# Attention values made transposed on two column tiles, with GpSimd scaling the probabilities

## The reference, cut to what matters

```python
h = x @ w_in                                   # 256 x 3080
prob = softmax(q @ k.T * hd**-0.5 + bias)      # or + c_t - c_s, causal
o = prob @ v                                   # per head, 256 x 64
return concat(o) @ w_out                       # 1024 x 1024
```

## Time and profile before

| | |
|---|---|
| median of 3 runs | 1023.72 us (1022.42 to 1024.78) |
| profiled execution, own time | 1023.21 us |
| its span | 1021.7 us |
| TensorE busy in the span | 1012.8 us (99%) |
| VectorE, ScalarE, GpSimd busy | 610.1, 448.5, 41.9 us |
| mean granted clock | 0.999 |

### The profile page before, as it was taken

One profiled execution on the slowest core, in us unless ns is written; L12 is line 12 of the kernel. 1 busy time (PEld: TensorE's weight loads), 2 busy tenths in 40 slices (PEclk: granted clock), 3 DMA queues, 4 the chain that ended last, 5 costly groups with the idle time before them and its releaser, 6 DMA issues.

```text
span 1021.7 us, 12789 instructions
## 1 busy us (share of the span) xinstructions
PE 1012.8 (99%) x4816; PEld 836.2 (82%) x4816; DVE 610.1 (60%) x716; ACT 448.5 (44%) x523; POOL 41.9 (4%) x55
## 2 busy tenths in 40 slices
PE   9999999999999999999999999999999999999998
PEld 7888888888888888888888888888887888888887
DVE  5655455776478745454677544545778864545574
ACT  5444344346473643434356343434344553434441
POOL 0400000100000000000010000000210100000010
PEclk9999999999999999999999999999999999999999
DMA  8875656355236766565539656564467676465531
GB/s 289 283 230 177 208 171 210 114 178 172 83 110 220 250 204 205 164 205 164 165 128 321 210 165 206 165 212 156 135 194 238 204 250 206 164 207 171 196 124 42
DMA packets 129683, 191.47 MB, mean 187 GB/s; under 512 B 5448, under 2 KB 95816, under 8 KB 129520
## 3 DMA queue, kind: packets, MB, share of 16 engines
q1 hardware_dynamic: 126432, 180.11, 53.9%
q0 software_dynamic: 2928, 10.61, 3.1%
q10 hardware_dynamic: 288, 0.26, 0.1%
HBM read 189.90 MB, written 1.06 MB: 187 GB/s over the span
## 4 chain that ended last, share of the span: by engine, by line
PE 93%; DVE 4%; DMA 1%; ACT 1%; issue 1%; SPq 0%; DVEq 0%; ACTq 0%
PE gu L388 19%; PE gu L390 19%; PE gu L389 19%; PE acc L388 10%; PE acc L390 10%; PE acc L389 10%; PE tp L466 4%; DVE g_lo L1118 2%; DMA rawB<-in_sgu_w_in 1%; ACT g_hi L830 1%; PE acc L653 1%; DVE t_tok L1514 0%; DVE xT_lo L1118 0%; DMA x_tok<-in_x 0%; DVE stage L1505 0%
## 5 line engine op out<-in xcount | busy, mean ns | idle before, releaser
L388 PE MATMUL gu<-g_hi,xT_hi 128*128 128x512 f32 x928 | 363.5, 392 | 1.2 <-DVE xT_lo L1118 1.1
L390 PE MATMUL gu<-g_hi,xT_lo 128*128 128x512 f32 x928 | 361.0, 389 | 0.0
L389 PE MATMUL gu<-g_lo,xT_hi 128*128 128x512 f32 x928 | 360.4, 388 | 0.0
L388 PEld LDWEIGHTS gu<-g_hi,xT_hi 128*128 128x128 f32 x928 | 174.3, 188 | 37.5 <-issue 2.4
L390 PEld LDWEIGHTS gu<-g_hi,xT_lo 128*128 128x128 f32 x928 | 174.2, 188 | 36.2
L389 PEld LDWEIGHTS gu<-g_lo,xT_hi 128*128 128x128 f32 x928 | 174.3, 188 | 34.8
L896 ACT ACTIVATE stage<-gu 128x256 f32<-128x256 f32 x88 | 33.7, 383 | 361.2 <-PE gu L390 361.1
L1118 DVE TENSOR_TENSOR g_lo<-rawA,g_hi 128x2048 fp32r<-128x2048 f32 (+2 forms) x66 | 141.5, 2145 | 78.4 <-ACT g_hi L830 78.3
L1118 DVE TENSOR_TENSOR g_lo<-rawB,g_hi 128x2048 fp32r<-128x2048 f32 (+1 forms) x64 | 141.0, 2203 | 18.1 <-ACT g_hi L830 18.1
L1244 DVE SCALAR_TENSOR_TENSOR stage<-stage,gu 128x256 f32<-128x256 f32 x88 | 37.0, 420 | 189.6 <-ACT stage L896 189.6
L388 PE MATMUL acc<-d_hi,hT_hi 128*128 128x512 f32 x352 | 144.8, 411 | 0.0
(11 more groups left out here) (181 smaller groups left out, 673.1 us busy)
## 6 DMA issues: line engine op xcount, KB each, us to landing
rawD<-in_ffn_w_down SPq DMA_DIRECT2D x44, 1024.0 KB, 4.9
rawA<-in_ffn_w_gate SPq DMA_DIRECT2D x42, 512.0 KB, 4.0
rawA<-in_ffn_w_up SPq DMA_DIRECT2D x42, 512.0 KB, 4.9
rawB<-in_ffn_w_gate SPq DMA_DIRECT2D x42, 512.0 KB, 4.4
rawB<-in_ffn_w_up SPq DMA_DIRECT2D x42, 512.0 KB, 5.5
rawA<-in_attn_w_in SPq DMA_DIRECT2D x12, 512.0 KB, 4.4
rawB<-in_attn_w_in SPq DMA_DIRECT2D x12, 512.0 KB, 4.9
rawA<-in_ple_w_gate SPq DMA_DIRECT2D x8, 512.0 KB, 4.7
```

The lines of the kernel that those rows point to most:

```text
L388: pe.matmul(dst, hi[b], w_hi[b], start=first and b == 0, stop=False)
L389: pe.matmul(dst, hi[b], w_lo[b], start=False, stop=False)
L390: done = pe.matmul(dst, lo[b], w_hi[b], start=False, stop=last and b == len(hi) - 1)
```

## The change

Four things change.

1. `values` works on a pair of heads at once and swaps the operands: v (64 columns) is stationary and the turned probabilities (128 columns) move, so the result stands transposed, head 2p in rows 0 to 63 and head 2p+1 in rows 64 to 127. It is 6 matmuls of 64x128 a pair, alternating between the two column tiles, where it was 6 of 128x64. The result goes straight into `oT_hi`, `oT_lo` (MoBA) and `xT_hi`, `xT_lo` (FoX) by `outputs`, so `group_out`, `o turn` and `oT` go, and with them 16 transposes on TensorE.
2. The row sums can then no longer be applied to the result. For each pair VectorE makes the reciprocals (`inverse`) and GpSimd multiplies the probabilities in place, two instructions a head, before TensorE turns them. `probs_turn` waits for GpSimd (`scaled`) and not for ScalarE (`p_ready`).
3. Where a product of h = 1 follows a transposition, it starts with 8 of its matmuls that need only `xT_hi` (`g_product_high_first`).
4. In sgu, VectorE's order around `gate_y` changes. `ATTN_ORDER` is rewritten to fit.

```diff
     ("g", 4, 0), ("probs", 2), ("probs", 3), ("scores", 2), ("exps", 2), ("turn", 3, 1), ("values", 1),
+    ("outputs", 0, 0), ("inverse", 2),
...
+        with ExitStack() as region:
+            oT_hi = sb("oT_hi", [P, HEADS, S], F32R, region)
+            oT_lo = sb("oT_lo", [P, HEADS, S], F32R, region)
...
+            def g_product_high_first(slot, dst, high_use, operand_wait):
+
+                tok = slice(P, 2 * P)
+                pe.wait_ge(tp_hi[0], high_use)
+                for b in range(4):
+                    pe.matmul(dst, xT_hi[:, b, tok], g_hi[:, slot, b, :], start=b == 0, stop=False)
+                    pe.matmul(dst, xT_hi[:, b, tok], g_lo[:, slot, b, :], start=False, stop=False)
+                operand_wait(0, 1)
+                for b in range(4):
+                    pe.matmul(dst, xT_lo[:, b, tok], g_hi[:, slot, b, :], start=False, stop=False)
+                operand_wait(1, 1)
+                g_piece(slot, 1, dst, 4, KB).then_inc(g_done, 1)
...
                     def probs_turn(n):
-                        pe.wait_ge(p_ready, n + 1)
+                        pe.wait_ge(scaled, n + 1)
...
-                        pe.matmul(o[0][:, oc], probsT[:, sl, 2 * P:3 * P], v_att[:, 0, vc],
-                                  start=True, stop=True)
-                        pe.matmul(o[1][:, oc], probsT[:, sl, 0:P], v_att[:, 0, vc], start=True, stop=False)
-                        pe.matmul(o[1][:, oc], probsT[:, sl, P:2 * P], v_att[:, 1, vc],
-                                  start=False, stop=True).then_inc(pv_done, 1)
+                        o = heads_out[g][p % 4 // 2]
+                        for q, keys, part in ((0, 0, 2), (1, 0, 0), (1, 1, 1)):
+                            for r in range(2):
+                                vc = slice(P * p + HD * r, P * p + HD * r + HD)
+                                done = pe.matmul(o[HD * r:HD * r + HD, at + P * q:at + P * q + P],
+                                                 v_att[:, keys, vc], probsT[:, r, P * part:P * part + P],
+                                                 start=keys == 0, stop=keys == q)
+                        done.then_inc(pv_done, 1)
...
+                        elif e[0] == "outputs":
+                            g, b = e[1:]
+                            src, hi, _ = outputs_of(g, b)
+                            act.wait_ge(pv_done, 4 * g + 2 * b + 2)
+                            copy(hi, src).then_inc(o_hi, 1)
...
+                        elif e[0] == "inverse":
+                            pair = slice(2 * e[1], 2 * e[1] + 2)
+                            dve.wait_ge(p_ready, 2 * e[1] + 2)
+                            dve.reciprocal(row_inv[:, :, pair], row_sum[:, :, pair]).then_inc(inverse_done, 1)
+                        elif e[0] == "outputs":
+                            g, b = e[1:]
+                            src, hi, lo = outputs_of(g, b)
+                            dve.wait_ge(o_hi, 2 * g + b + 1)
+                            low(lo, src, hi).then_inc(tok_ready, 1)
...
                     lo_g(g0 + 4, 0)
                     gate_y(0)
-                    lo_g(g0 + 4, 1)
                     xT_low(0, v0)
                     biased(7, 3)
+                    lo_g(g0 + 4, 1)
+                    lo_g(g0 + 5, 0)
                     gate_y(1)
-                    for part in range(2):
-                        lo_g(g0 + 5, part)
+                    lo_g(g0 + 5, 1)
                     residual(0, 0, r0, (g_done, 2 * (g0 + 4) + 1))
...
+                if ln == 0:
+                    for n in range(2 * HEADS):
+                        pool.wait_ge(inverse_done, n // 2 + 1)
+                        for q, cols in ((1, slice(0, S)), (0, slice(S, S + P))):
+                            done = pool.tensor_scalar(probs[:, n % 2, cols], probs[:, n % 2, cols],
+                                                      row_inv[:, q, n:n + 1], None, ALU.mult)
+                        done.then_inc(scaled, 1)
```

More of the change, by code:

```diff
@@ L66 @@
-    ("g front", 5, 0), ("probs", 6), ("probs", 7), ("values", 2), ("turn", 4, 1), ("g back", 5, 0), ("causal", 4),
-    ("values", 3), ("scores", 4), ("exps", 4), ("group out", 0), ("causal", 5),
+    ("outputs", 0, 0), ("inverse", 2),
+    ("g", 4, 1), ("probs", 4), ("probs", 5), ("scores", 3), ("exps", 3), ("turn", 4, 0), ("inverse", 3),
+    ("g front", 5, 0), ("turn", 4, 1), ("values", 2), ("probs", 6), ("probs", 7), ("g back", 5, 0), ("causal", 4),
+    ("values", 3), ("scores", 4), ("outputs", 0, 1), ("exps", 4), ("causal", 5), ("inverse", 4),
@@ L68 @@
     ("g front", 5, 1), ("probs", 8), ("probs", 9), ("g back", 5, 1), ("scores", 5), ("exps", 5), ("causal", 6),
[L69 to L72, removed]
@@ L73 @@
-    ("out front", 0, 0, 2), ("w_next", 0), ("probs", 14), ("probs", 15), ("w_next", 1),
-    ("out front", 0, 2, 4), ("values", 7),
-    ("out front", 1, 0, 2), ("oT", 0), ("out front", 1, 2, 4), ("oT", 1)]
+    ("proj", 0), ("p_copy", 0), ("inverse", 5), ("w_out", 0), ("values", 4), ("w_low", 0), ("proj", 1), ("w_out", 1),
+    ("p_copy", 1), ("probs", 10), ("probs", 11), ("w_out", 2), ("scores", 6), ("exps", 6), ("proj", 2), ("p_copy", 2),
+    ("inverse", 6), ("causal", 7), ("w_out", 3), ("values", 5), ("w_low", 1), ("proj", 3), ("p_copy", 3),
@@ L80, in attn_tp_uses @@
+    ("probs", 12), ("probs", 13), ("scores", 7), ("outputs", 1, 0), ("exps", 7), ("inverse", 7), ("w_low", 2), ("values", 6),
+    ("w_low", 3), ("out piece", 0, 0, 4), ("probs", 14), ("probs", 15), ("w_next", 0), ("w_next", 1),
+    ("out piece", 1, 0, 4), ("out piece", 0, 4, 6), ("values", 7), ("outputs", 1, 1), ("out piece", 1, 4, 6)]
 def attn_tp_uses():
@@ L763, in y_wait @@
[L763 to L765 removed]
+                    after = (t0 + 6 + HEADS, t0 + 6 + HEADS + 1)
                 if kind == "sgu":
@@ L816, in _ @@
                             x_turn()
[L817 to L821 removed]
+                        if kind == "attn" and j == 0:
+                            pe.wait_ge(tok_ready, x0 + 4)
+                            g_piece(out0 % 2, h, acc[h][:, j, :], 6, KB, attn_out).then_inc(g_done, 1)
+                        elif kind == "attn":
+                            g_product(out0 + j, (out0 + j) % 2, h, acc[h][:, j, :], None, between, src=attn_out)
+                        else:
+                            g_product(out0 + j, (out0 + j) % 2, h, acc[h][:, j, :],
+                                      y_wait if n % 2 == 0 else None, between,
+                                      front=out_front_done if n == 2 else None)
+                    use, high_use = after, B["v"] + (3 if kind == "attn" else 4)
                     def half1_block(j, x0=x0 + 4, use=use):
```

147 lines of the change are left out of this document (56 added, 91 removed).

## The result

The changed kernel takes 1045.41 us in the median of 5 runs (1044.7 to 1047.74), the kernel before, beside it on the same chip, 1023.43 us in 5 runs. The ratio is 1.0224, interval 1.0213 to 1.0234: 22 us slower. I had forecast 1023.8 and a range up to 1028.0, so the prediction was wrong: one chain, TensorE waiting for GpSimd, was priced far too low.

A forecast was written before the change was run, and what follows sets the result against it. TensorE was taken to bound the kernel, busy 1012.8 of 1021.7 us. Gains of 8.1 against 6.2 added in attention and 2.1 in sgu gave +0.2, so 1023.8 us as the median, range 1019.0 to 1028.0.

The forecast's parts named there:

- the price of GpSimd's multiplication: In attention, two multiplications a head priced like GpSimd's affine selects: 0.69 us a head, 0.9 possible.
- The price by itself: In attention, TensorE's waits for reciprocals and GpSimd with nothing in GpSimd's way, and for the last outputs: 4.7 us added.
- The sentence on the second head: In attention, the second head comes 0.69 us later, half covered by the first head's turning of 0.35: 0.3 a pair.
- The port: In attention, GpSimd waits for VectorE's two-input subtractions: 1.0 us in pair 7, 0.2 to 0.3 in pairs 5 and 6, 1.5 together.
- The clock: TensorE's clock falling in the long wait, named as a sign that the forecast is wrong; no size in the sum.
- Values: In attention, transposed values on two column tiles at the scores' pace: 0.5 us less a pair, 4.0 in all.
- rival 4: In attention's values, the column tiles do not run side by side and save nothing: 1027.8 us; chance 0.10.
- Transposes: On TensorE, 16 transposes go, 8 of which cost 0.93 us: 1.9 us less.
- sgu: In sgu, two waits go (1.3 us) but the `rawB` load starts 2.6 later, a wait of some 3.5: net loss 2.1.
- rival 2: In sgu, the load lands in time and both waits go, -1.3 in place of +2.1: 1020.4 us; chance 0.10.
- The waits behind `xT_lo`: At the start of attn and two ffns, eight matmuls needing only `xT_hi` cover the subtraction: 3 x 0.50 = 1.5 us less.
- Rival 3: In attention, each GpSimd instruction waits for one subtraction, 0.9 us a head: 1028.7 us, with half 1026.2; chance 0.20.

The follow-up runs named there:

- e3: The changed kernel without GpSimd's multiplications, the division by the row sums left out: 1020.29 us, ratio 0.9971.
- e11: The changed kernel with VectorE's attention subtractions held back until the pair before is multiplied, and TensorE multiplying extra products while it waits: 1034.90 us, ratio 1.0111.
- e6: The changed kernel with VectorE's subtractions in attention held back until GpSimd has multiplied the pair before: 1040.06 us, ratio 1.0150.
- e5: The changed kernel with TensorE multiplying extra products into the bank of the coming turn while it waits for GpSimd: 1040.34 us, ratio 1.0169.
- e2: The kernel before with only the products that start with the matmuls needing `xT_hi` alone: 1022.64 us, ratio 0.9995.
- e12: The changed kernel with VectorE's order in sgu as before: 1042.71 us, ratio 1.0194.
- e10: The changed kernel with VectorE multiplying the probabilities, the old sgu order and two places of attention's order changed: 1019.27 us, ratio 0.9959.

## Why the prediction was wrong

**The step that failed** is the price of GpSimd's multiplication: "The nearest are its affine selects of the same shapes, 0.398 for 128x256 and 0.295 for 128x128: 0.69 a head", and with it "above it a price of 0.9 a head is possible". It is 1.53 a head, 2.2 times as much. The mechanism stood in the text, that a late GpSimd holds TensorE ahead of the turnings, and so did the failure ("wrong if GpSimd costs much above 0.9 a head, if TensorE's clock falls in the long wait"). The size did not. A row of another operation on the same engine is no bound on the price from above; I treated 0.9 as one, on no row. The Trainium skill (GPSIMD Engine Reference, "3.1 Elementwise — side-by-side cycle accounting") has 769 ns for 512 elements in its best loop, 1.5 ns an element; my estimate of 0.8 a head was worked out from that, with two starts that it has no time for. The Trainium skill calls this loop the best case, and this case's trace lies above it: from 128 to 256 columns the instruction grows by 0.321 us (605 to 926 ns), 2.5 ns a column.

**What followed from it.** The forecast had attention 6.2 us above a version with nothing between exponentials and turnings. Measured against e3 it is 24.4 us in the trace, and 26 by the ratios. The parts, by the ratios:

- *The price by itself*, forecast 4.7, is 14.3 us by e11 against e3, the late low parts with it. In pair 4 I had 2.0 and the waits are 2.21 and 0.93. Pairs 0 to 3, where I had at most 0.3 each, have 0.76, none, 0.29, and 0.84 with 0.93 at this price alone (e6); pair 0's 2.95 in the changed kernel is for the most part the port. The sentence on the second head, that its lateness is half covered by a turning of 0.35, falls with the price too: the second head comes 1.5 later, and in four pairs (2, 4, 5 and 7) 0.93 of it is seen as a second wait.
- *The port*, 7.6 us by e6 and 5.9 from e5 to e11, forecast 1.5. "So a GpSimd instruction that starts during such a subtraction ends after it" was right, and so was the place, pair 7; but I took 1.0 there and its four instructions take 1.9 longer. And I looked only at the `w_low` halves in pairs 5 to 7: pairs 0 to 2 have a subtraction of 128x2048 within GpSimd's work too, which costs them 1.6 to 2.1 each. At 0.69 a head pair 0 would have been done 1.4 behind 245.61, before the subtraction at 247.14. The Trainium skill (SBUF — State Buffer, "SBUF: two separate sides") has this lock, for whoever starts first, and e6 agrees with it for GpSimd behind VectorE: without overlap every pair costs 2.98 to 3.13. For VectorE behind GpSimd this trace does not agree: a subtraction that began just behind a GpSimd instruction of 0.93 took only 0.28 longer (last section).
- *The clock*, 5.6 us by e5 and 4.0 from e6 to e11, which I had named and put at nothing. Five of the seven groups of waits in the trace were followed by products at 0.43 us instead of 0.23.

**What was right.** Values: 4.0 us forecast, 4.0 measured (10.66 to 6.66); rival 4 is dead. Transposes: 1.9 forecast, 1.64. sgu: a net loss of 2.1 from a load issued 2.6 us later; measured 2.4 on the kernel before, with the load 2.5 us later within the phase (797.57 - 750.72 against 776.03 - 731.70), and a wait of 2.73 instead of 3.5; what I left out is the lower clock behind it. So rival 2 is dead. The waits behind `xT_lo` went as the text said, but for 0.5 and not 1.5 us (e2, whose interval reaches from a gain of 1.5 to a loss of 0.4), since the ffn behind sgu gave back 1.0. All gains together were 8.1 in the text; e3's 3.0, with the sgu loss of 2.4 added back, shows 5.4.

**The rivals and the chances.** Rival 3 named the way it went, and stopped at 1028.7, since it took the same price. No case carried a price of twice the row's, so nothing in the range could reach 1045. It should have: the operation had no row, the factor turned out to be 2.2, and the term was 16 heads in series with the engine that bounds.

**What stays open.** How the 11.6 us of clock and port divide exactly: by the ratios e5 and e6 sum to 13.2 and e11 gives 11.6, within their intervals. And when the clock falls. Single runs that lie low have the higher clock: the run of e6 that lies 3 us or more below its others (1035.92) has a mean granted clock of 0.997, they 0.992 to 0.995. The lowest of e12 (1038.17) is the one with the trace: its attention is 2.4 us shorter than in the changed kernel's, with 0.7 less of waits and the clock at 0.94 and 0.87 where that read 0.88 and 0.83. The size of a wait does not decide it alone: 0.71 with 0.93 was followed by the lower clock and 1.22 with 0.93 was not, in one trace.

## What to carry to other kernels

Before work goes to an engine between a producer and the engine that bounds, ask for its price from a row of the same operation; without one, let the range hold well over twice the nearest row (2.2 times here), and count the price once for each link of the chain and not only for the first. Then the waits have interest: most groups of waits, of 1.6 us and more together, were followed here by some 3 us at the lower clock, all in all about 1 us more for 3 us of wait (4.0 to 5.6 on 14.8). Where VectorE can take the work in its gaps, 0.25 us an instruction there beats 0.6 to 0.9 on an idle GpSimd; the gain of this change (values and transposes, 5.6 us in the trace) was real, and most of it (4.2 us by e10's ratio) came through with VectorE for the factors, the old order in sgu and two places of attention's order changed.

## What the runs showed of the hardware

- GpSimd's tensor_scalar in place in f32: 0.93 us for 128x256 and 0.60 for 128x128 with a column of scalars, 0.85 and 0.53 with a constant; VectorE 0.35 and 0.28, and 0.25 each when four follow one another. GpSimd's affine selects of the same shapes take 0.40 and 0.30: operations of one shape differ by a factor of two and more.
- VectorE passes a waiting GpSimd: at 319.00 two subtractions of 1.2 us ran one behind the other (2.33 for both), while GpSimd's first multiplication, started at 319.18, ended behind both, after 2.86 us instead of 0.93. The other way round the wait is short: a subtraction of 128x2048 began at 257.53, just behind a GpSimd instruction of 128x256 that had begun at 257.5 and took its usual 0.93, and took 2.56 instead of 2.28, so 0.28 longer and not 0.9. GpSimd's next instruction, of 128x128, then took 2.19 instead of 0.60 and ended behind the subtraction. (Spans on GpSimd are rough.)

```profile
257.53 2.56 DVE L1147 TENSOR_TENSOR g_lo<-rawA,g_hi 128x2048 fp32r<-128x2048 f32 x1 [1.63 <-ACT g_hi L862]
```

- Two column tiles of 64 columns with 128 moving: 12 records in 0.80 us, 0.07 each, where transposes of 128 moving columns take 0.12 each; so they overlap.
- Products of TensorE into a bank that nobody reads, made while it waits, kept the granted clock at 1.00 through attention (e5) and gave 5.1 to 5.6 us back.
